# A ring of nine weight places read in place by experts in groups of three, and gate times sigmoid made before the up product's last step

## The chip, the cores and the metric

The kernel runs on one core of a Trainium2 chip. The metric is device time in microseconds of one execution; lower is better. The core has five engines with instruction streams of their own: TensorE (PE in the profile, with its weight loads as PEld), VectorE (DVE), ScalarE (ACT), GpSimd (POOL) and SyncE (SP), which here starts every transfer. Sixteen DMA engines move the data. Engines wait for each other through semaphores.

## The reference, cut to what matters

One layer: a gated delta-rule mixer and a state-space mixer side by side, an output projection, a residual, then a mixture of 32 experts over 256 tokens of width 1024, each token going to 4 experts. The change touches the experts, which are most of the time:

```python
def block_step(out, inp):                  # MoE_BLOCK rows of one expert e
    toks, gw, e = inp
    xb = t[toks]
    a = jnp.minimum(xb @ w_gate[e] + b_gate[e], SWIGLU_LIMIT)
    b = jnp.clip(xb @ w_up[e] + b_up[e], -SWIGLU_LIMIT, SWIGLU_LIMIT)
    hid = a * jax.nn.sigmoid(SWIGLU_ALPHA * a) * (b + 1)
    y = hid @ w_down[e] + b_down[e]
    return out.at[toks].add((y * gw[:, None]).astype(out.dtype)), None
```

All weights are float32, 1024 x 1024 each, three matrices for an expert.

## The kernel before, in words

Everything ahead of the experts (modulation, projections, the two mixers, the output projection, router) takes the first 427 us or so. The scratch memory is one tensor, `arena`, and `lay_out_sbuf` gives each name its place in it; places of names that are not alive together overlap.

The experts run in **turns**. A turn is a block of up to 64 rows (`SLOT`) of one expert. Every expert has at least one turn; one with more than 64 rows has further ones. The list of turns (`intab`) is made on the chip by VectorE (mark `table`), so the loops read numbers from it: entries from `BLOCKS` on hold, for each expert, the last turn of that expert. For these inputs there are 34 turns for the 32 experts: two experts have a second turn.

An expert's weights come as six **pieces** of 2048 KB: gate rows 0 to 511, up rows 0 to 511, gate rows 512 to 1023, up rows 512 to 1023, and the two halves of down. `ring` has a place for each piece, so piece n of every expert lands in place n. SyncE's loop (`pieces`, L507 to L519) waits, for each expert and piece in order, until TensorE has used that piece in the previous expert's last turn (mark `piece`, n), and then starts the transfer (L493). TensorE waits for its landing before the 16 matmuls that read it.

A turn on TensorE (`block_of_rows`, L1148 to L1193) has this order: the gate and up biases (L1156, 4 matmuls); four pieces of 16 matmuls each (L1163); the scatter of the previous turn's output into the accumulators (L1133, 8); after VectorE's `hid`, four transposes of it (L1172); the gather of the next turn's rows (L1124, 48); two transposes of the gates (L1180); the down bias (L1184, 2); two pieces of 16 (L1190). VectorE in a turn (L2239 to L2271): the selection masks of the turn ahead, then the limit on the gate product into `a` (L2259), the limit on the up product (L2261), `(up + 1) * a` (L2263), and, when ScalarE's sigmoid is there (L1544), the product with it (L2266, mark `hid`). ScalarE also copies the transposed hidden rows (L1546), the gathered rows (L1548), the gates (L1550) and the turn's output (L1552) out of the matmul banks.

TensorE, VectorE and ScalarE each have three loops over turns with one copy of the turn's code in each: turns 2 to 16, up to 15 tested turns of which `n_more` (here 2) are run and the others skipped, and the last 16. TensorE has the first turn apart. So TensorE's code holds the turn four times.

Ahead of the experts, SyncE loads the first pieces as their places come free: pieces 0 to 2 of expert 0 after the mark `mixT`, piece 3 after `low`, then the nine small copies of the biases, then pieces 4 and 5 after the last output projection.

After the last turn VectorE, ScalarE and SyncE do the last norm, the residual and the store.

Of the kernel before, what the change touches and what calls it, by code (L numbers as in the profile page):

```python
# [40 lines left out]
ARENA = 53100  # L41
LEVELS = (2, 4, 8, 16, 32)
PIECES = 6

# [43 lines left out]
class Lane:  # L88
# [23 lines left out]
    def at(self, who, *step, back=0):  # L112

        name, value = self.book.old.get((who,) + step) or self.book.new.get((who,) + step) or (f"{who}_dry", 1)
        assert self.book.dry or (who,) + step in self.book.old, (who, step)
        if name in self.book.per_old:
            value = (self.turn - back) * self.book.per_old[name] + value
        return self.sems(name), value
# [22 lines left out]
def lay_out_sbuf():  # L141
# [3 lines left out]
    def put(base, *items):  # L145
        for name, n in items:
# [6 lines left out]
    keep = put(0, ("const", NCONST), ("x", 2 * D), ("rows", 4 * D), ("cols", 8 + 20 * 5 + 8),  # L153
               ("small", 720), ("gates", 2304))
# [21 lines left out]
    put(at["WT"][0], ("yt", 4 * 512), ("mixT", KT * 256))  # L176
    put(at["kdS"][0], ("wout", KT * D))

    e = put(keep, ("h", 2 * D), ("hp", 3 * D), ("wr", 256), ("bias", 3 * 512), ("acc", 2 * D), ("hid", 6 * 512))
    assert at["wr"][0] >= at["k_tm"][0] and at["bias"][0] + at["bias"][1] <= at["xs_tm"][0]  # L180
    put(at["hid"][0], ("mix", 2 * D))
    put(e, ("hT", KT * 256))
    e = put(e, ("xcT", 512), ("hidT", 512), ("y", 512), ("GT", 256), ("Sg", 256))
    put(e, ("Sb", 64), ("route", 1500), ("ring", PIECES * 4096))
# [6 lines left out]
def layer_program(nc, book, x, ctx, consts, cc, b_ada, w_ada, wfm, wz, wsm, cols, small, wrow, w_out, w_router,  # L191
                  w_gate, w_up, w_down, b_gate, b_up, b_down, out):
    stack = ExitStack()
    with stack:
# [27 lines left out]
        rows = view(area("rows"), 4, D)  # L222
# [29 lines left out]
        brow = [xin[:, 0], rows[:, 3], xin[:, 1], area("modp", 0, D)]  # L252
# [76 lines left out]
        bst = area("v_tm", 0, D)  # L329
        b_parts = [area("v_tm", D, 512).bitcast(BF16), area("v_tm", D + 512, 512).bitcast(BF16), area("b_tm", 512, 512).bitcast(BF16)]  # L330
        dskip_eye = area("XT0", 512, 512)
        x1, hm = view(area("hid", 0, 2 * D), 2, D), view(area("h"), 2, D)
# [4 lines left out]
        acc = view(area("acc"), 2, D)  # L337
        xcT = view(area("xcT"), KT, SLOT)
        hid = view(area("hid"), 6, 512)
# [5 lines left out]
        ring = view(area("ring"), PIECES, 4, D)  # L345
        r_at = [0]
# [33 lines left out]
        passed = view(area("rows", 0, BLOCKS * 32), BLOCKS, 32)  # L380
# [26 lines left out]
        def _(sp):  # L407
# [38 lines left out]
            load("wrow", area("rows", 0, 3 * D), wrow)  # L446
# [2149 lines left out]
```

## Time and profile before

| | before |
|---|---|
| runs, us | 1397.33, 1401.47, 1409.28 |
| median | 1401.47 |
| span of the profiled execution | 1396.9 |
| TensorE busy, share of the span | 90% |
| VectorE busy | 29% |
| ScalarE busy | 19% |
| GpSimd busy | 9% |
| DMA moved | 458.59 MB, mean 328 GB/s |
| mean granted TensorE clock | 0.962 |

The profile shows one execution. The span is the time from the first to the last recorded instruction; the profiled execution has no time of its own beside it, and the lowest of the three runs is 0.4 us above the span. Busy time of TensorE counts matmuls that overlap, so a high share doesn't say that the engine is at its limit. The chain of waits is the list of steps that ended last, each with what it had to wait for; it tells who sets the pace in a stretch. Throughput in a stretch tells whether the transfers are at their limit.

### The profile page before, as it was taken

Reading aid. Unit: us, or ns where it says so; the run is one execution under the profiler, and the core shown is the slowest. Engines: PE = TensorE matmul, PEld = TensorE weight load, DVE = VectorE, ACT = ScalarE, POOL = GpSimd, SP = SyncE. Lnnn points to the kernel's source line nnn. Section 1 sums busy time; section 2 is a strip of 40 time slices with the busy share of each in tenths; the row PEclk is TensorE's granted clock in tenths of the full one; section 3 lists DMA queues with packets and bytes.
Section 4 is the critical chain, followed back from the end, with each engine's and each line's share of the span. In section 5 each row is a group of like instructions: output and inputs, shape, how many; then the busy total and the mean of one; then the engine's idle time right before and its main releaser. Section 6 shows DMA issues by size and latency. Waiting matters only on the chain.

```text
span 1396.9 us, 24933 instructions
## 1 busy us (share of the span) xinstructions
PE 1252.0 (90%) x10197; PEld 555.7 (40%) x10198; DVE 402.7 (29%) x896; ACT 260.1 (19%) x501; POOL 121.0 (9%) x168
## 2 busy tenths in 40 slices
PE   5999898568989999988999889988989999999996
PEld 2445445466654333333333333333333333333432
DVE  1265469817855121111111111111111112111112
ACT  2421432336041111111111111100000101100102
POOL 0211540185000000000000000000000000000000
PEclk9999999769988999999999999999999999999998
DMA  9958010010476999999999999999999699969994
GB/s 354 397 182 316 31 61 30 5 34 31 180 308 254 426 426 428 427 428 427 426 426 426 426 428 427 427 427 425 426 426 420 268 427 426 426 266 426 428 427 179
DMA packets 48135, 458.59 MB, mean 328 GB/s; under 512 B 4417, under 2 KB 4817, under 8 KB 22737
## 3 DMA queue, kind: packets, MB, share of 16 engines
q1 hardware_dynamic: 48080, 457.81, 79.1%
q8 instruction: 42, 0.69, 0.2%
q14 instruction: 13, 0.10, 0.0%
HBM read 456.15 MB, written 1.05 MB: 327 GB/s over the span
## 4 chain that ended last, share of the span: by engine, by line
PE 54%; DMA 34%; DVE 7%; issue 2%; ACT 1%; POOL 1%; DVEq 0%; SPq 0%; POOLq 0%; ACTq 0%
DMA arena<-in_w_up 33%; PE bank L1163 21%; PE bank L1190 8%; PE bank L673 7%; PE bank L1055 2%; PE bank L1124 2%; PE bank L584 2%; PE bank L544 1%; DVE arena L1737 1%; PE bank L1172 1%; DVE arena L2266 1%; DVE arena L2263 1%; DVE arena L2261 1%; DMA arena<-in_x 1%; PE bank L904 1%
## 5 line engine op out<-in xcount | busy, mean ns | idle before, releaser
L1163 PE MATMUL bank<-arena 128*64 128x512 f32 x2176 | 484.6, 595 | 43.7 <-DMA arena<-in_w_up 22.5
L1163 PEld LDWEIGHTS bank<-arena 128*64 128x64 f32 x2176 | 150.1, 136 | 359.3 <-issue 263.9
L1190 PE MATMUL bank<-arena 128*64 128x512 f32 x1088 | 239.2, 592 | 0.0
L2259 DVE TENSOR_SCALAR arena<-bank 128x512 f32<-128x512 f32 x34 | 23.6, 693 | 403.3 <-PE bank L1163 403.3
L1190 PEld LDWEIGHTS bank<-arena 128*64 128x64 f32 x1088 | 75.9, 136 | 140.5 <-issue 138.0
L673 PE MATMUL bank<-arena 128*128 128x512 f32 (+1 forms) x320 | 123.7, 540 | 0.0
L673 PEld LDWEIGHTS bank<-arena 128*128 128x128 f32 x320 | 60.7, 195 | 58.2 <-issue 55.3
L2190 DVE TENSOR_SCALAR arena<-arena 96x64 bf16<-96x64 f32 x35 | 8.8, 251 | 224.6 <-PE bank L1190 224.6
L1133 PE MATMUL bank<-arena 64*128 64x512 f32 x280 | 69.6, 614 | 0.8 <-ACT arena L1552 0.8
L1124 PE MATMUL bank<-arena 128*128 128x64 bf16 x1680 | 62.8, 198 | 1.1 <-DVE arena L2186 1.1
L1124 PEld LDWEIGHTS bank<-arena 128*128 128x128 bf16 x1680 | 62.9, 118 | 1.2 <-DVE arena L2186 1.2
L1544 ACT ACTIVATE arena<-arena 128x512 f32<-128x512 f32 x34 | 21.5, 632 | 219.0 <-DVE arena L2259 218.8
L1552 ACT ACTIVATE arena<-bank 128x512 f32<-128x512 f32 x34 | 20.4, 600 | 224.3 <-PE bank L1190 224.3
L1737 DVE SCALAR_TENSOR_TENSOR arena<-arena 128x512 f32<-128x512 f32 (+1 forms) x80 | 59.2, 740 | 2.8
L1544 ACT ACT_TABLE_LOAD x16 | 20.5, 1283 | 197.4 <-DVE arena L2259 197.4
L2261 DVE TENSOR_SCALAR arena<-bank 128x512 f32<-128x512 f32 x34 | 23.6, 693 | 113.1 <-PE bank L1163 113.1
L1546 ACT ACTIVATE arena<-bank 128x512 f32<-128x512 f32 x34 | 20.5, 604 | 168.6 <-PE bank L1172 168.6
L1133 PEld LDWEIGHTS bank<-arena 64*128 64x128 f32 x280 | 24.1, 185 | 45.7 <-issue 40.8
L1172 PE MATMUL bank<-arena 128*128 128x128 f32 x136 | 25.5, 310 | 11.4 <-DVE arena L2266 11.4
L1172 PEld LDWEIGHTS bank<-arena 128*128 128x128 f32 x136 | 19.1, 210 | 39.5 <-DVE arena L2266 39.5
L2248 DVE TENSOR_SCALAR arena<-arena 128x128 f32<-128x128 f32 x68 | 20.6, 346 | 42.8 <-issue 28.4
L1055 PE MATMUL bank<-arena 128*128 128x512 f32 x64 | 31.1, 643 | 0.0
(352 smaller groups left out, 1029.2 us busy)
## 6 DMA issues: line engine op xcount, KB each, us to landing
arena<-in_w_gate SPq DMA_DIRECT2D x64, 2048.0 KB, 22.5
arena<-in_w_up SPq DMA_DIRECT2D x64, 2048.0 KB, 24.1
arena<-in_w_down SPq DMA_DIRECT2D x64, 2048.0 KB, 22.0
arena<-in_w_ada SPq DMA_DIRECT2D x12, 2048.0 KB, 9.7
arena<-in_wfm SPq DMA_DIRECT2D x20, 512.0 KB, 3.4
arena<-in_wz SPq DMA_DIRECT2D x4, 1024.0 KB, 14.3
arena<-in_w_out SPq DMA_DIRECT2D x2, 2048.0 KB, 8.3
arena<-in_x SPq DMA_DIRECT2D x2, 1024.0 KB, 7.6
```

Of the source, the lines that this page charges most:

```text
L584: last = mm(ps[z_bank[m][t]], xmT[:, k, base:base + 128], ada[:, m, k, :], start=(k == 0), stop=(k == KT - 1))
L673: last = mm(dst, win[:, i % 3, k, :], cols_, start=(k == 0), stop=(k == KT - 1))
L1055: last = mm(ps[2 + 2 * t + c_], mixT[:, k, 128 * t:128 * t + 128], wout[:, k, 512 * c_:512 * c_ + 512], start=(k == 0), stop=(k == KT - 1))
L1124: last = mm(ps[7][:, SLOT * k:SLOT * k + SLOT], hparts[:, s_, t, 512 * (k // 4) + k % 4:512 * (k // 4) + 512:4], Sb[:, t, :], start=(n == ...
L1133: last = mm(ps[3 + 2 * t + c_], GT[r, t, :], ysb[r, :], start=first, stop=last_one)
L1163: last = mm(ps[m][64 * c_:64 * c_ + 64, :], xcT[:, k, :], ring[:, 2 * h_ + m, k % 4, 512 * c_:512 * c_ + 512], start=False, stop=(k == KT ...
L1172: last = nc.tensor.transpose(unit(ps[0], k), hid[:, 4, k:512:4], ident)
L1190: last = mm(ps[2][64 * c_:64 * c_ + 64, :], hidT[:, k % 4, 64 * (k // 4):64 * (k // 4) + 64], ring[:, 4 + h_, k % 4, 512 * c_:512 * c_ + 5 ...
L1544: f(hid[:, 1], hid[:, 0], ACT.Sigmoid, scale=ALPHA).then_inc(*L.mark("sig"))
L1737: v.scalar_tensor_tensor(out=dst, in0=src, scalar=convw[:, wi, tap:tap + 1], in1=dst, op0=ALU.mult, op1=ALU.add).then_inc(*L.mark("conv", i))
L2259: v.tensor_scalar(hid[:, 0], ps[0][:, :], LIMIT, None, ALU.min).then_inc(*L.mark("a"))
L2261: v.tensor_scalar(hid[:, 2], ps[1][:, :], LIMIT, -LIMIT, ALU.min, ALU.max).then_inc(*L.mark())
```

## The change: what it does

- **Ring.** There are nine places for pieces (`PLACES`): the six of `ring` and three more (`ahead0` to `ahead2`). Two of the three overlap memory that is used up to the router (`h`, `hT`; `rows`, `mix`), so the layout is rearranged: the hidden rows, the small tiles of a turn, the bias parts and the table's mask move onto constants and columns that are dead by then; `acc` and the final rows are in `ring`.
- **In place.** Piece n of expert e lands in place (6e + n) mod 9. Three experts (18 pieces) make two whole rounds, so the places repeat every three experts (`PHASES`). SyncE's and TensorE's loops go over groups of three experts (10 `GROUPS`, experts 2 to 31) with the three written out, and each reads its places directly.
- **Waits.** A piece waits for the use of the piece nine earlier: pieces 0 to 2 of an expert for pieces 3 to 5 of the expert two before, pieces 3 to 5 for pieces 0 to 2 of the expert before.
- **First pieces.** Piece 0 of expert 0 is started right after the router's weights, pieces 1 and 2 after VectorE's marks `Oss` and `gdn`, piece 0 of expert 1 after `mixT` and `Yss`; pieces 1 and 2 of expert 1 after the router's last use of the memory under them. Further ones in the loop.
- **TensorE's code.** A first turn of each expert is written out; its further turns are a test, and inside it a loop over k = 2 to 4 with a test each. TensorE reads two numbers of the table for an expert instead of one for a turn. Its three old loops go. The code holds the turn ten times, six of them in the loop over groups. VectorE and ScalarE keep their loops.
- **Sigmoid.** VectorE multiplies the limited gate product with the sigmoid before it waits for the last up piece; behind that piece come the up limit and one product, not two.
- The store reads `final`, and the load of the three norm rows is split in two.

The diff, cut to its core:

```diff
+PLACES = 9
+PHASES = 3
+GROUPS = (E_N - 2) // PHASES
...
-    e = put(keep, ("h", 2 * D), ("hp", 3 * D), ("wr", 256), ("bias", 3 * 512), ("acc", 2 * D), ("hid", 6 * 512))
...
-    put(e, ("Sb", 64), ("route", 1500), ("ring", PIECES * 4096))
+    e = put(keep, ("mix", 2 * D), ("h", 2 * D), ("hT", KT * 256), ("route", 1500), ("bias", 3 * 512), ("hp", 3 * D))
+    at["ahead2"] = (at["rows"][0] + 2 * D, 4096)
+    at["ahead1"] = (at["h"][0], 4096)
+    e = put(e, ("ahead0", 4096), ("ring", PIECES * 4096))
...
+    put(at["ring"][0] + 3 * 4096, ("wout", KT * D), ("yt", 4 * 512), ("mixT", KT * 256))
...
-            def piece(n, expert):
+            def piece(n, first, group=0):
 
                 m, c = order[n]
-                src = halves[m][bass.ds(expert, 1), c].rearrange("e p n -> p (e n)")
-                sp.dma_start(ring[:, n].rearrange("p k n -> p (k n)"), src).then_inc(sems(f"in_ring{n}"), 16)
+                place = (PIECES * first + n) % PLACES
+                src = halves[m][first:E_N:PHASES][bass.ds(group, 1), c].rearrange("e p n -> p (e n)")
+                sp.dma_start(places[place], src).then_inc(sems(f"in_place{place}"), 16)
+
+            piece(0, 0)
+            sp.wait_ge(*L.at("dve", "Oss", 1))
+            piece(1, 0)
+            sp.wait_ge(*L.at("dve", "gdn", 1))
+            piece(2, 0)
             sp.wait_ge(*L.at("pe", "mixT", 0, 1))
-            for n in range(3):
-                piece(n, 0)
+            sp.wait_ge(*L.at("dve", "Yss", 1))
+            piece(0, 1)
...
+            sp.wait_ge(*L.at("pe", "logit", 1))
+            sp.wait_ge(*L.at("act", "hparts", 0, 1))
+            sp.wait_ge(*L.at("dve", "rest", 0))
+            sp.wait_ge(*L.at("pool", "rest", 1))
+            piece(1, 1)
+            sp.wait_ge(*L.at("dve", "h", 1))
+            sp.wait_ge(*L.at("dve", "hparts", 1))
+            piece(2, 1)
...
-            def pieces(blocks, expert):
-                L.begin_turn(blocks)
-                for n in range(PIECES):
-                    sp.wait_ge(*L.at("pe", "piece", n))
-                    piece(n, expert)
+            def later_pieces(first, group, before):
+
+                for n in range(PLACES - PIECES, PIECES):
+                    sp.wait_ge(*L.at("pe", "piece", n - (PLACES - PIECES), turn=before))
+                    piece(n, first, group)
+
+            def first_pieces(first, group, two_before):
+
+                for n in range(PLACES - PIECES):
+                    sp.wait_ge(*L.at("pe", "piece", n + (PLACES - PIECES), turn=two_before))
+                    piece(n, first, group)
 
             sp.wait_ge(*L.at("dve", "table"))
-            with sp.Fori(1, E_N) as i:
-                pieces(sp.value_load(intab[0:1, bass.ds(i + (BLOCKS - 1), 1)], min_val=1, max_val=BLOCKS - 1), i)
+            later_pieces(1, 0, sp.value_load(intab[0:1, BLOCKS:BLOCKS + 1], min_val=1, max_val=BLOCKS - 1))
+            with sp.Fori(0, GROUPS) as g:
+                last = [last_turn_of(g * PHASES + n) for n in range(PHASES + 1)]
+                for n in range(PHASES):
+                    first_pieces(n + 2, g, last[n])
+                    later_pieces(n + 2, g, last[n + 1])
...
+            def further_blocks(before, last, first, group):
+
+                with pe.If(last > before + 1):
+                    with pe.Fori(2, SEQ // SLOT + 1) as k:
+                        with pe.If(last > before + (k - 1)):
+                            block_of_rows(before + k, first, group)
+                L.turn = None
...
-            with pe.Fori(2, HALF_E + 1) as i:
-                block_of_rows(i, expert_of(i))
...
-            with pe.Fori(0, MAX_MORE) as k:
-                with pe.If(n_more > k):
-                    block_of_rows(k + HALF_E + 1, expert_of(k + HALF_E + 1))
-            with pe.Fori(HALF_E + 1, E_N + 1) as i:
-                block_of_rows(n_more + i, expert_of(n_more + i))
+            last = last_turn_of(0)
+            further_blocks(0, last, 0, 0)
+            before, last = last, last_turn_of(1)
+            block_of_rows(before + 1, 1, 0)
+            further_blocks(before, last, 1, 0)
+            with pe.Fori(0, GROUPS) as g:
+                for n in range(PHASES):
+                    before, last = last_turn_of(g * PHASES + n + 1), last_turn_of(g * PHASES + n + 2)
+                    block_of_rows(before + 1, n + 2, g)
+                    further_blocks(before, last, n + 2, g)
...
-                v.tensor_scalar(hid[:, 0], ps[0][:, :], LIMIT, None, ALU.min).then_inc(*L.mark("a"))
+                v.tensor_scalar(hid[0], ps[0][:, :], LIMIT, None, ALU.min).then_inc(*L.mark("a"))
+                dve.wait_ge(*L.at("act", "sig"))
+                v.tensor_tensor(hid[3], hid[0], hid[1], ALU.mult).then_inc(*L.mark())
                 dve.wait_ge(*L.at("pe", "piece", 3))
-                v.tensor_scalar(hid[:, 2], ps[1][:, :], LIMIT, -LIMIT, ALU.min, ALU.max).then_inc(*L.mark())
+                v.tensor_scalar(hid[2], ps[1][:, :], LIMIT, -LIMIT, ALU.min, ALU.max).then_inc(*L.mark())
                 dve.wait_ge(*L.own())
-                v.scalar_tensor_tensor(out=hid[:, 3], in0=hid[:, 2], scalar=1.0, in1=hid[:, 0], op0=ALU.add, op1=ALU.mult).then_inc(*L.mark())
-                dve.wait_ge(*L.at("act", "sig"))
-                dve.wait_ge(*L.own())
-                v.tensor_tensor(hid[:, 4], hid[:, 3], hid[:, 1], ALU.mult).then_inc(*L.mark("hid"))
+                v.scalar_tensor_tensor(out=hid[4], in0=hid[2], scalar=1.0, in1=hid[3], op0=ALU.add, op1=ALU.mult).then_inc(*L.mark("hid"))
```

## Rows read from the trace of the kernel before

**Rows 1.** The page: busy tenths and throughput in 40 slices of 34.9 us.

```profile
DMA  9958010010476999999999999999999699969994
GB/s 354 397 182 316 31 61 30 5 34 31 180 308 254 426 426 428 427 428 427 426 426 426 426 428 427 427 427 425 426 426 420 268 427 426 426 266 426 428 427 179
```

**Rows 2.** Chain of waits, start and length in us: two turns paced by transfers.

```profile
543.43 3.68 PE bank L1163 x16
547.12 25.73 DMA arena<-in_w_up
572.90 3.68 PE bank L1163 x16
```

**Rows 3.** Chain of waits: turns 1 to 3, then 23 to 34 in part.

```profile
427.71 13.75 PE bank L1163 x64
...
453.93 13.76 PE bank L1163 x64
...
480.17 13.76 PE bank L1163 x64
...
1074.59 3.68 PE bank L1163 x16
...
1090.73 13.76 PE bank L1163 x64
...
1116.96 13.76 PE bank L1163 x64
...
1195.66 13.76 PE bank L1163 x64
1209.44 25.54 DMA arena<-in_w_up
1235.03 3.68 PE bank L1163 x16
...
1251.17 13.76 PE bank L1163 x64
...
1375.03 6.90 PE bank L1190 x32
```

**Rows 4.** Transfers started by SyncE before the experts, around turn 1 and around turn 24.

```profile
365.26 0.35 SPq L413 DMA_DIRECT2D arena<-in_w_router  x1
376.79 0.34 SPq L493 DMA_DIRECT2D arena<-in_w_gate  x1
...
431.62 0.35 SPq L493 DMA_DIRECT2D arena<-in_w_gate  x1
...
1057.43 3.77 SPq L493 DMA_DIRECT2D arena<-in_w_down  x2
1094.36 0.34 SPq L493 DMA_DIRECT2D arena<-in_w_gate  x1
```

**Rows 5.** Last uses of the memory under the places ahead, GpSimd and VectorE.

```profile
415.87 2.09 POOL L2505 TENSOR_TENSOR arena<-arena 128x1024 f32<-128x1024 f32 x1 [9.31 <-ACT arena L1521]
...
419.70 2.35 DVE L2168 TENSOR_TENSOR arena<-arena 128x1024 bf16<-128x1024 f32 x2
```

**Rows 6.** Timeline of turn 2 behind its last up piece.

```profile
466.49 0.63 ACT L1544 ACTIVATE arena<-arena 128x512 f32<-128x512 f32 x1
467.60 1.99 PE L1133 MATMUL bank<-arena 64*128 64x512 f32 x8
467.72 0.69 DVE L2261 TENSOR_SCALAR arena<-bank 128x512 f32<-128x512 f32 x1 [2.63 <-PE bank L1163]
469.17 0.69 DVE L2266 TENSOR_TENSOR arena<-arena 128x512 f32<-128x512 f32 x1
469.92 0.75 PE L1172 MATMUL bank<-arena 128*128 128x128 f32 x4 [0.34 <-DVE arena L2266]
```

**Rows 7.** Timeline and windows: TensorE's start of turn 19, and its granted clock.

```profile
949.57 1.07 PE L1156 MATMUL bank<-arena 96*64 96x512 bf16 x4 [6.64 <-DVE arena L2186]
...
950.64 14.72 PE bank L1163 x64
...
950.00:953.00 3.00, 3.00 (x12) 1.10 (x10) 0.00 (x0) 0.00 (x0) 0.00 (x0) 0.59 1.03 437
```

**Rows 8.** Code queue (count, MB, share): whole span, 0 to 427, 903 to 910 us.

```profile
q8 instruction: 42, 0.69, 0.2%
...
q8 instruction: 36, 0.59, 0.6%
...
q8 instruction: 1, 0.02, 1.0%
```

**Rows 9.** All queues in 480 to 903 us; busy us (x instructions) before 427.

```profile
q1 hardware_dynamic: 12397, 180.57, 100.6%
...
0.00:427.00 427.00, 356.87 (x4613) 216.59 (x4614) 240.53 (x493) 142.69 (x303) 121.01 (x168) 0.89 0.43 158
```

**Rows 10.** Chain of waits: the last up piece of turns 17, 18 and 21.

```profile
871.36 25.73 DMA arena<-in_w_up
897.14 3.68 PE bank L1163 x16
900.83 26.34 DMA arena<-in_w_up
927.21 3.68 PE bank L1163 x16
...
1015.63 3.68 PE bank L1163 x16
```

More of the change, by code:

```diff
@@ L345, in layer_program @@
         ring = view(area("ring"), PIECES, 4, D)
+        places = [area("ring", 4096 * i, 4096) for i in range(PIECES)] + [area(f"ahead{i}") for i in range(PLACES - PIECES)]
         r_at = [0]
@@ L1065, in _ @@
                     at_ = 2 * (KT * j + k)
-                    last = mm(ps[4][:, at_:at_ + 2], rows[:, row, 128 * k:128 * k + 128], ident[:, 0:2], start=True, stop=True)
+                    last = mm(ps[4][:, at_:at_ + 2], rows[row][:, 128 * k:128 * k + 128], ident[:, 0:2], start=True, stop=True)
             last.then_inc(*L.mark("rcols"))
@@ L1146, in _, with place_of, weights, landed @@
             L.stage("moe")
-            def block_of_rows(turn, expert, first=False):
+            def place_of(n, first):
+                return (PIECES * first + n) % PLACES
+            def weights(n, first):
+                return places[place_of(n, first)].rearrange("p (k n) -> p k n", k=4)
+            def landed(n, first, group):
+                return sems(f"in_place{place_of(n, first)}"), group * (2 * 16) + 16 * ((PIECES * first + n) // PLACES + 1)
+            def block_of_rows(turn, first, group, start=False):
                 L.begin_turn(turn)
@@ L1159, in block_of_rows @@
                     for m in range(2):
-                        pe.wait_ge(sems(f"in_ring{2 * h_ + m}"), expert * 16 + 16)
+                        w = weights(2 * h_ + m, first)
+                        pe.wait_ge(*landed(2 * h_ + m, first, group))
                         for k in range(4 * h_, 4 * h_ + 4):
                             for c_ in range(2):
-                                last = mm(ps[m][64 * c_:64 * c_ + 64, :], xcT[:, k, :], ring[:, 2 * h_ + m, k % 4, 512 * c_:512 * c_ + 512],
+                                last = mm(ps[m][64 * c_:64 * c_ + 64, :], xcT[:, k, :], w[:, k % 4, 512 * c_:512 * c_ + 512],
                                           start=False, stop=(k == KT - 1))
@@ L1167, in block_of_rows @@
                 pe.wait_ge(*L.at("act", "y", back=1))
-                scatter(first).then_inc(*L.mark("back"))
+                scatter(start).then_inc(*L.mark("back"))
                 pe.wait_ge(*L.at("dve", "hid"))
                 for k in range(4):
-                    last = nc.tensor.transpose(unit(ps[0], k), hid[:, 4, k:512:4], ident)
+                    last = nc.tensor.transpose(unit(ps[0], k), hid[4][:, k:512:4], ident)
                 last.then_inc(*L.mark("hidT"))
@@ L1186, in block_of_rows @@
                 for h_ in range(2):
-                    pe.wait_ge(sems(f"in_ring{4 + h_}"), expert * 16 + 16)
+                    w = weights(4 + h_, first)
+                    pe.wait_ge(*landed(4 + h_, first, group))
                     for k in range(4 * h_, 4 * h_ + 4):
@@ L1751, in row_out @@
                     dve.wait_ge(*L.own())
-                    v.scalar_tensor_tensor(out=rows[:, row, r], in0=b_, scalar=1.0 if which == 2 else 0.0, in1=rows[:, row, r],
+                    v.scalar_tensor_tensor(out=rows[row][:, r], in0=b_, scalar=1.0 if which == 2 else 0.0, in1=rows[row][:, r],
                                                  op0=ALU.add, op1=ALU.mult).then_inc(*L.mark("scaled", use))
```

73 lines of the change are left out of this document (40 added, 33 removed).

## The prediction, made before the changed kernel ran

> **What bounds the kernel now.** I read first the slices of the page: up to 427 us the transfers are mostly idle, and from slice 13 on they run at 426 to 428 GB/s, but for two slices at 268 and 266 [rows 1]. So the experts are mostly paced by weights. Then the chain of waits. In [rows 2] the last up piece of one turn starts 29.47 us after that of the turn before, and between them stands a transfer: six pieces in 29.47 us, 4.91 us each. In [rows 3] turn 24 starts 26.23 us before turn 25 (1116.96 - 1090.73) with only TensorE in the chain: TensorE alone needs 26.23 us for a turn, 3.24 less than its weights. TensorE keeps that pace from turn 24, the second one of its expert, to turn 28. In turn 29 the transfers are the limit again: from turn 28 to turn 30 it takes 1251.17 - 1195.66 = 55.51 us, 3.05 more than two turns of 26.23. From turn 30, again a second one, TensorE sets the pace to the end. So a turn without new weights builds a reserve, which then lasts about four turns.
>
> Why not longer is in SyncE's rows: after expert 22's last pieces at 1057.43 and 3.77 us later, nothing is started until 1094.36 [rows 4], since all six places are held until the second turn has used the first. The slices of 268 and 266 GB/s are (427 - 268)/427 x 34.9 = 13.0 and 13.2 us without transfers.
>
> **The change, part by part.**
>
> Three more places, filled ahead of turn 1. Before, the first place comes free at 431.62 [rows 4], with six pieces in memory. After, nine are there if those of expert 1 land in time. Their last conditions end at 415.87 + 2.09 = 417.96 and 419.70 + 2.35 = 422.05 [rows 5]; with 4.91 us of transfer each on idle queues (the page moves next to nothing there) the last lands near 430. The first piece starts right after 365.26 and not at 376.79 [rows 4]. The place that frees at 431.6 then takes the tenth piece and not the seventh, so all later landings come 3 x 4.91 = 14.7 us earlier, as long as transfers are the limit. That is so up to turn 23: TensorE alone would be through it at 427.7 + 23 x 25.9 = 1023, the weights of [rows 3] less 14.7 say 1059.9 for the last up piece that started at 1074.59. **-14.7.**
>
> Turns 24 to 34. In turn 24 the transfers have three free places for expert 23's first pieces, 14.7 us of work, and the fourth frees with the first piece's matmuls, some 4 us into it, so the 13 us of idle go. That does not count as 13 us: TensorE was already the limit there. What goes is the wait in turn 29, for the reserve is then 25.9 us, and the five turns 25 to 29 use 5 x 3.6 = 18. **-3.05.** At turn 30 it is the same; its idle time too is behind TensorE's pace.
>
> The sigmoid. In turn 2 the scatter ends at 467.60 + 1.99 = 469.59, VectorE's last product at 469.86, and the transposes start at 469.92, with 0.34 of idle [rows 6]. The sigmoid ended at 467.12, so the moved product runs to about 467.9, delays the up limit by 0.2, and `hid` is there at 469.3. The scatter now ends last. So one 0.69 us instruction less gives only the 0.3 us down to the scatter; in turns paced by TensorE 12 times (end of 23, 24 to 34). **-3.6.** If ScalarE were late, the product would sit in front of the up limit and cost instead; the sigmoid ends 0.5 us ahead of the last up piece, with a table load in it (later turns have none).
>
> SyncE. The waits moved in front of piece 1 of expert 0 up to `low` are marks that TensorE itself needs before `low`, so piece 3 and the nine bias copies aren't later; the queue ahead of them is shorter, since three pieces start up to 11 us earlier. Four table reads at a group's start delay a start while nine pieces are outstanding or landed: 0. If that cover went, in the last turns, a start would be some 2 us late with pieces landing 8 us ahead of use.
>
> TensorE's holes at the change of loops. Turn 19 begins with 6.64 us of idle, after two run and 13 skipped tests, and its four pieces take 14.72 and not 13.76, its biases 1.07, at a granted clock of 0.59 [rows 7]. That hole goes, but lies in a stretch paced by transfers: 0. VectorE and ScalarE keep theirs, with 14 us until they are needed. In its place TensorE gets two more tests in each second turn; 13 cost at least 6.64, so 0.5 each; **+1.0** for turn 24 and 30.
>
> TensorE's code. This is the unknown. Code comes in transfers of its own: 42 of 16 KB over the span, 36 of them before 427 us, where TensorE ran 4613 + 4614 instructions: one for 256 instructions [rows 8, 9]. From 480 to 903 us the loop of one turn (164 matmuls and as many weight loads, 328) goes round 14 times and no code is loaded [rows 9]. The new loop has six copies, 1968 instructions and the waits: 8 or 9 such transfers, a third of them jumped over. No row shows a loop of that size. Two costs.
> First, on the weight stream: the one code transfer in 903 to 910 us [rows 8] made the next last up piece 0.6 us late (26.34 for 25.73), and the two between turns 19 and 21 cost nothing: 1015.63 - 927.21 = 88.42 is three times 29.47 [rows 10]. If every group reloads nine, 66 up to turn 23, and they spread over the 16 engines, that is 66 x 16 KB at 427 GB/s = 2.5 us; if none, 0. I take **+1.5.**
> Second, TensorE waiting for code at a jump. Lower end 0: turn 3, entered by a jump back and a table read, starts 26.24 us after turn 2; turn 2, entered by straight code, 26.22 after turn 1 [rows 3]. Upper end: the nearest hole is turn 19's, 6.6 of idle and (14.72 - 13.76) + (1.07 - 0.6) = 1.4 of slow clock, 8.0 at the end of each group that TensorE paces, after experts 22, 25 and 28: 24. I take **+6**, two of eight each: nearer to the loop that reloads nothing, because those 0.02 us say that something covers a short wait there.
>
> Here a page speaks against the change. Only the trace's loops of 328 instructions run without a reload. The Trainium skill, Runtime: NRT & Kernel Launch, Instruction fetch mechanics, gives TensorE a first-in-first-out instruction memory of 128 KiB, filled in blocks of 16 KiB, and says that a taken branch whose target isn't in it stalls for a fetch. The trace agrees on the blocks (0.69 MB in 42), not on a window that holds the next block only. By that page the new loop would not fit and would stall at every group's end, which is the first rival's sum.
>
> **Sum.** -14.7 - 3.05 - 3.6 + 1.0 + 1.5 + 6 = -12.9 us: a span of 1384.0 against 1396.9. The median of the runs shown is 1401.47, 4.6 above that span, so **1388.6**. For the range of this case alone, the code term between 0 and 14: 1382.6 to 1396.6.
>
> **Rivals.**
>
> 1. *The loop's code is fetched again for each group, and TensorE waits for it.* For: six copies, where the trace shows only one staying. Against: the stretch before 427 us runs through 36 code transfers at that engine's full rate. The code term is then 24, and 2.5 for 1.5: 1396.9 - 12.9 + 18 + 1 = 1403.0, as a median 1407.6. No change. Even half of it would hide in turns up to 23, where each group has 3 x 3.6 = 10.7 us of slack.
>
> 2. *Slower: code transfers on the weight stream.* If nine a group all fell on the same of the 16 engines, each would cost the whole 0.6 us of [rows 10], and they would add: 66 x 0.61 = 40 us up to turn 23, against the 1.5 in the sum, so 1401.47 - 12.9 + 38.5 = 1427. It turns the sign from (12.9 + 1.5) / 66 = 0.22 us each on. Against it: the two that cost nothing.
>
> 3. *The reserve does not arise.* If the places under the router's memory were filled late, or the first free place had to wait, the stream would stay as before, and the 14.7 are lost from the sum: -12.9 + 14.7 = +1.8, 1403.3, no change. Against: 5 us of idle transfers at least ahead of 431.6.
>
> 4. *More than forecast.* No code term on either side (-7.5) and turn 1 starting 2 us or more earlier, as the bias copies land earlier: 1379 or less.
>
> **How the numbers follow.** Forecast 0.60, rival 1 0.21, rival 2 0.09, rival 3 0.06, rival 4 0.04. A measurement of this kernel tells about 1% from no change, so faster means below 1387.5 and slower above 1415.5. The forecast case lies below 1387.5 while the code term is under 4.9; I give that two thirds of it, 0.40, for the low end has the only row of a loop. Rival 4 adds 0.04: faster 0.44. Slower has most of rival 2, 0.08, and 0.01 of rival 1 with longer holes. The rest is same: 0.47. The range takes in the forecast case, rivals 1 and 3 and what rival 4 gives just below it, and leaves out most of rival 2: 1377 to 1408.
>
> **What would show it.** Nine pieces landed before 432 us, and the last up piece of every turn from about 10 to 23 starting 29.5 us after the one before, that of turn 23 near 1060. No slice of the experts' stretch below 400 GB/s until the last. From turn 24 turns of 25.9 us without a transfer in the chain. Transposes right behind the scatter. In the code queue, 42 transfers or so if the loop stays, 120 or more if it does not; then idle time of TensorE ahead of L1156 once in three experts says what a wait costs. The prediction is wrong if those holes exceed 5 us each, if the stretch up to turn 23 has turns above 30 us, or if turn 1 starts more than 3 us off 427.5.

## The result: slower, 1456.4 us, because TensorE waits for code at the end of every group

| | before | after |
|---|---|---|
| median of four runs, us | 1399.4 (1394.01 to 1409.28) | 1456.37 (1449.69 to 1458.65) |
| ratio, with its 95% interval | | 1.0396 [1.0343, 1.0448] |
| span of the profiled execution | 1396.9 | 1454.5 |
| mean granted TensorE clock | 0.962 | 0.921 |
| transfers in the code queue | 42 | 140 |

The forecast was 1388.6, the range 1377 to 1408.

First the page after, its slices (now 36.4 us each), its code queue and the chain by engine. They answer to [rows 1] and [rows 8].

```profile
PEclk9999999669969998998989989899899999899898
...
GB/s 357 366 208 270 44 58 16 33 5 80 358 232 420 425 424 422 426 424 404 424 421 401 426 394 427 421 389 425 392 425 209 371 425 424 388 170 427 354 343 30
...
q8 instruction: 140, 2.29, 0.7%
...
PE 83%; issue 8%; DVE 5%; ACT 2%; DMA 1%; POOL 1%; DVEq 0%; SPq 0%; POOLq 0%; ACTq 0%
```

The weights no longer set the pace: DMA has 1% of the chain, and from slice 13 on the throughput is below the steady 427 of before nearly everywhere, more so toward the end. "Issue", time in which the engine waited for nothing the profile shows, has 8%. The list of groups says where (busy us, mean ns | idle us ahead, releaser):

```profile
L1210 PE MATMUL bank<-arena 96*64 96x512 bf16 x136 | 25.3, 457 | 104.5 <-issue 102.5 <-ACTq L1605 1.0 <-DVE arena L2253 0.6
```

L1210 is the biases, a turn's first matmuls (L1156 before). Now one group of three experts in the chain, from one group's first turn to the next one's (start, length in us):

```profile
576.66 15.95 PE bank L1218 x64
...
604.69 13.74 PE bank L1218 x64
...
630.87 13.74 PE bank L1218 x64
...
656.30 0.61 ACT arena L1619
656.91 10.51 issue
667.42 1.07 PE bank L1210 x4
668.49 16.11 PE bank L1218 x64
```

Behind the third expert nothing runs for 10.51 us; then the biases take 1.07 and the gate and up matmuls 16.11, where they take 0.43 and 13.74 inside the group. All nine group ends look so: 10.07, 10.51, 10.70, 10.73, 11.04, 10.68, 4.97, 11.16 and 11.44 us. The 4.97 is the end whose last expert has a second turn, and a hole of 2.93 stands before expert 2's turn. The granted clock says what the slow matmuls are (windows: length, busy us of PE, PEld, DVE, ACT and POOL, granted clock, DMA share, GB/s):

```profile
566.00:575.00 9.00, 0.00 (x0) 0.00 (x0) 0.00 (x0) 0.00 (x0) 0.00 (x0) 0.57 0.99 408
576.00:580.90 4.90, 4.90 (x16) 1.61 (x14) 0.00 (x0) 0.00 (x0) 0.00 (x0) 0.50 1.01 421
581.00:584.00 3.00, 3.00 (x16) 0.98 (x14) 0.00 (x0) 0.00 (x0) 0.00 (x0) 1.00 1.02 431
```

In the hole the grant falls to the lower level, one half (0.57 is the mean of a stretch that begins before the fall), and it stays there for the first 4 us or so of the next turn's gate and up matmuls; from 581 on it is full. No engine is busy in the hole. The trace also records TensorE's jump instructions, which no row of the page counts: at a group's end the jump over the second turn's copy takes 5.9 to 6.7 us and the jump back 7.2 to 7.7, where a jump whose target is at hand takes 0.21 to 0.24. (At the end of expert 22 there is only a jump back, of 6.1 us.) TensorE itself is idle for 11.16 us (timeline):

```profile
667.42 1.07 PE L1210 MATMUL bank<-arena 96*64 96x512 bf16 x4 [11.16 <-issue]
```

The chain gives the first 0.6 us of them to ScalarE's copy of the turn's output (L1619), but this runs beside the first jump and inside a group holds no turn up, so all 11.16 belong to the code. The two jumps take 13.5: matmuls already handed to the engine run for 4.4 us beside the first one, and 1.9 us, most of it table reads, stand between the second one and the biases. Inside a group the jumps over the copy take 1.3 to 3.3 us and hold TensorE up by 0.8 us at most.

A group takes 668.49 - 576.66 = 91.83 us. Three turns without a hole are 3 x 25.83 = 77.5, so a group's end costs 14.3: 11.2 of idle TensorE, 2.9 of slow clock, and the rest in the start of the third expert's turn (630.87 - 604.69 = 26.18), behind a jump of 2.8 us. The 18 pieces of a group need 18 x 4.91 = 88.4 by their transfers. TensorE, with its stops, is slower than the weights by 3.4 us in every group, and the reserve of nine places is never used up.

The rest of the change shows as forecast. In turn 2, behind the last up piece (answers to [rows 6]):

```profile
470.58 0.63 ACT L1611 ACTIVATE arena<-arena 128x512 f32<-128x512 f32 x1
471.24 0.69 DVE L2328 TENSOR_TENSOR arena<-arena 128x512 f32<-128x512 f32 x1 [2.07 <-ACT arena L1611]
...
471.69 1.99 PE L1175 MATMUL bank<-arena 64*128 64x512 f32 x8
471.85 0.69 DVE L2330 TENSOR_SCALAR arena<-bank 128x512 f32<-128x512 f32 x1
...
472.57 0.69 DVE L2332 SCALAR_TENSOR_TENSOR arena<-arena 128x512 f32<-128x512 f32 x1
...
473.61 0.75 PE L1227 MATMUL bank<-arena 128*128 128x128 f32 x4
```

The product with the sigmoid (L2328) is done as the scatter (L1175) starts, the last product (L2332) ends at 473.26, and the transposes (L1227) start at 473.61 with no idle time ahead of them. SyncE starts the ninth piece at 423.62 and goes on as places come free (answers to [rows 4]):

```profile
366.94 0.43 SPq L509 DMA_DIRECT2D arena<-in_w_gate  x1
...
423.62 0.33 SPq L509 DMA_DIRECT2D arena<-in_w_gate  x1
435.43 0.33 SPq L509 DMA_DIRECT2D arena<-in_w_up  x1
```

**One measure for what follows.** The first gate matmul of turn 1 starts anywhere from 423.9 to 436.8 us in the profiled executions of these kernels, also in ones whose code is the same up to there but for a skipped block. A gain of a few us is lost in that. So profiled executions are compared by the span less that start: before 1396.9 - 427.71 = 969.2, after 1454.5 - 429.63 = 1024.9.

### The profile page after: what moved, and what is told of

The parts are those of the page before. It is cut to its first block, busy times and chain, and to the rows that moved or that the text cites. A ratio compares the mean times of both kernels' runs of the same rounds, so it can differ in the third digit from the quotient of the medians.

```text
span 1454.5 us, 24935 instructions
## 1 busy us (share of the span) xinstructions
PE 1270.3 (87%) x10197; PEld 568.6 (39%) x10198; DVE 401.8 (28%) x896; ACT 259.9 (18%) x501; POOL 120.8 (8%) x168
## 4 chain that ended last, share of the span: by engine, by line
PE 83%; issue 8%; DVE 5%; ACT 2%; DMA 1%; POOL 1%; DVEq 0%; SPq 0%; POOLq 0%; ACTq 0%
PE bank L1218 34%; PE bank L1246 16%; PE bank L715 7%; PE bank L1175 4%; PE bank L1166 4%; PE bank L1097 2%; PE bank L626 2%; PE bank L1227 2%; PE bank L1210 2%; PE bank L586 1%; DVE arena L1804 1%; PE bank L1239 1%; PE bank L946 1%; DMA arena<-in_x 1%; PE bank L1235 1%
## 5 line engine op out<-in xcount | busy, mean ns | idle before, releaser
L1218 PE MATMUL bank<-arena 128*64 128x512 f32 x2176 | 494.1, 613 | 0.0
L1218 PEld LDWEIGHTS bank<-arena 128*64 128x64 f32 x2176 | 160.9, 142 | 317.3 <-issue 313.1
L1246 PE MATMUL bank<-arena 128*64 128x512 f32 x1088 | 239.2, 592 | 0.0
L2326 DVE TENSOR_SCALAR arena<-bank 128x512 f32<-128x512 f32 x34 | 23.6, 693 | 496.4 <-PE bank L1218 496.4
L1246 PEld LDWEIGHTS bank<-arena 128*64 128x64 f32 x1088 | 75.9, 136 | 140.6 <-issue 138.0
L1210 PE MATMUL bank<-arena 96*64 96x512 bf16 x136 | 25.3, 457 | 104.5 <-issue 102.5
L715 PEld LDWEIGHTS bank<-arena 128*128 128x128 f32 x320 | 61.0, 195 | 58.2 <-issue 55.2
L1175 PE MATMUL bank<-arena 64*128 64x512 f32 x280 | 69.6, 614 | 0.8 <-ACT arena L1619 0.8
L1619 ACT ACTIVATE arena<-bank 128x512 f32<-128x512 f32 x34 | 20.4, 599 | 224.3 <-PE bank L1246 224.3
L1210 PEld LDWEIGHTS bank<-arena 96*64 96x64 bf16 x136 | 6.5, 119 | 130.0 <-issue 116.2
L1175 PEld LDWEIGHTS bank<-arena 64*128 64x128 f32 x280 | 24.1, 185 | 45.8 <-issue 31.1
L2328 DVE TENSOR_TENSOR arena<-arena 128x512 f32<-128x512 f32 x34 | 23.6, 694 | 47.3 <-ACT arena L1611 47.3
L586 PE MATMUL bank<-arena 128*32 128x512 f32 x192 | 25.6, 659 | 6.0 <-DMA arena<-in_w_ada 6.0
## 6 DMA issues: line engine op xcount, KB each, us to landing
arena<-in_w_down SPq DMA_DIRECT2D x64, 2048.0 KB, 14.3
```

Of the source, the lines that this page charges most:

```text
L586: last = mm(ps[bank][32 * g:32 * g + 32, :], sct[:, k, :], ada_of(use)[:, k, :], start=k < 4, stop=(k >= 4))
L715: last = mm(dst, win[:, i % 3, k, :], cols_, start=(k == 0), stop=(k == KT - 1))
L1175: last = mm(ps[3 + 2 * t + c_], GT[r, t, :], ysb[r, :], start=first, stop=last_one)
L1210: mm(ps[m][64 * c_:64 * c_ + 64, :], selb[0:96, :], bias[0:96, m, 512 * c_:512 * c_ + 512], start=True, stop=False)
L1218: last = mm(ps[m][64 * c_:64 * c_ + 64, :], xcT[:, k, :], w[:, k % 4, 512 * c_:512 * c_ + 512], start=False, stop=(k == KT - 1))
L1246: last = mm(ps[2][64 * c_:64 * c_ + 64, :], hidT[:, k % 4, 64 * (k // 4):64 * (k // 4) + 64], w[:, k % 4, 512 * c_:512 * c_ + 512], start= ...
```

## The experiments

My theory: the long loop over groups costs TensorE a wait for code at each group's end, and all else of the change works as forecast. Its rivals: the nine places or their transfers are slow in themselves; it is the jumps as such, not the loop's size; the waits are long only because the code's transfer stands behind the weights' in the DMA queues. (Letters in a quoted expectation are that expectation's own.)

### e1_three: all of the change, with TensorE's loop at half its size

```diff
+            def all_blocks(before, last, first, group):
+
+                with pe.Fori(before + 1, last + 1) as turn:
+                    block_of_rows(turn, first, group)
...
-                    before, last = last_turn_of(g * PHASES + n + 1), last_turn_of(g * PHASES + n + 2)
-                    block_of_rows(before + 1, n + 2, g)
-                    further_blocks(before, last, n + 2, g)
+                    all_blocks(last_turn_of(g * PHASES + n + 1), last_turn_of(g * PHASES + n + 2), n + 2, g)
```

> The changed kernel with TensorE's turns of an expert in one loop whose bounds are read from the table, so the loop over groups holds the turn three times and not six; places, waits, transfers and the sigmoid stay. Theory (TensorE waits for its code at the end of each group, because six copies don't stay in its instruction memory): code transfers fall from 140 to about 50, no jump is longer than 0.3 us, the holes of 10 to 11 us go, and the sum of the prediction without a code term is left plus the 1.9 us by which turn 1 starts later: a span of about 1379, ratio to the kernel before 0.985 to 0.99. Rival (the new places or the new order of transfers cost the time): holes or long turns stay, 1440 or more. Second rival (the code was all of the loss, but the reserve brings nothing): 1397.

Measured: 1376.1 us, ratio to the kernel before 0.9829 [0.9804, 0.9855]: 1.7% less than the kernel before, 5.5% less than after. In the list of groups the idle time ahead of L1210 falls from 104.5 us to 1.1, and the code queue holds 44 transfers:

```profile
L1210 PE MATMUL bank<-arena 96*64 96x512 bf16 x136 | 20.4, 379 | 1.1 <-ACTq L1608 1.0
...
q8 instruction: 44, 0.72, 0.2%
```

The chain shows what the nine places do when TensorE isn't held up:

```profile
433.52 13.73 PE bank L1218 x64
...
1025.63 39.60 DMA arena<-in_w_up
1065.27 3.65 PE bank L1218 x16
...
1081.02 13.73 PE bank L1218 x64
...
1106.85 13.73 PE bank L1218 x64
...
1339.33 6.01 PE bank L1218 x22
```

The weights set the pace up to the last up piece of turn 23, 631.75 us after turn 1; before it was 1074.59 - 427.71 = 646.88 [rows 3], so the three places bring 15.1. From there no transfer is in the chain to the end, and a turn takes 25.83. From turn 1 to the end it is 946.3 us, 22.9 less than before. The nine places are not slow, and what e1 does differently is TensorE's loop alone (its size, and that no unused copy is jumped over; e7 to e10 below separate the two).

### e2_six_ring6: the long loop alone

```diff
-            with pe.Fori(2, HALF_E + 1) as i:
...
+            with pe.Fori(0, 10) as g:
+                for n in range(3):
+                    before, last = last_turn_of(g * 3 + n + 1), last_turn_of(g * 3 + n + 2)
+                    block_of_rows(before + 1, g * 3 + n + 2)
+                    further_blocks(before, last, g * 3 + n + 2)
```

> The kernel before with the changed kernel's TensorE loop alone: groups of three experts, six copies of the turn in the loop; ring of six, old waits, old sigmoid order. Theory (code): the holes of 10 to 11 us at each group's end and a slow start of the next turn appear, about 13 us for ten groups against 9 us of slack a group that transfers give, and 15 us of lost lead at the end of each second turn, so 1440 to 1475 and about 140 code transfers. Rival (the ring is what costs): 1395 to 1405.

Measured: 1465.85 us, ratio 1.0479 [1.0446, 1.0512], 140 code transfers. The kernel before, with nothing but the six copies, has after's holes (chain):

```profile
565.47 10.44 issue
575.91 1.07 PE bank L1156 x4
576.98 15.43 PE bank L1163 x64
```

From turn 1 it is 1464.0 - 423.86 = 1040.1 us, 70.9 more than before: the loop alone does the harm. It is also 15.3 more than after, and 33 x 0.4 = 13 of that is the old order of the sigmoid (below), paid in every turn where TensorE sets the pace. That leaves some 2 us for the nine places: with this loop they bring next to nothing.

### e3_sigmoid and e5_three_oldsig: the order of the sigmoid, alone and taken out

```diff
+                dve.wait_ge(*L.at("act", "sig"))
+                v.tensor_tensor(hid[:, 3], hid[:, 0], hid[:, 1], ALU.mult).then_inc(*L.mark())
                 dve.wait_ge(*L.at("pe", "piece", 3))
                 v.tensor_scalar(hid[:, 2], ps[1][:, :], LIMIT, -LIMIT, ALU.min, ALU.max).then_inc(*L.mark())
```

e3 puts this into the kernel before; e5 puts the old order into e1.

> The kernel before with only the sigmoid's product moved ahead of the wait for the last up piece. Theory: 0.3 us less in each turn that TensorE paces (16 of 34: turns 1 to 4, 19, 20, 24 to 28, 30 to 34), of which those up to turn 20 are given back to the transfers: 2 to 4 us less, ratio 0.997 to 0.9985. Rival: nothing measurable because the scatter ends last anyway: 1.000. If the product delays the up limit when ScalarE is late: slower by up to 0.7 us a turn.

> The kernel with three copies (e1_three), with the old order of VectorE's part: the product with the sigmoid last. Theory: the turns that TensorE paces (24 to 34 and the first ten) take 0.3 to 0.4 us more, the others nothing; 11 turns behind the stretch paced by transfers make 3 to 5 us: 1380 beside 1376. Rival (the order is covered here too): no difference to e1_three.

Measured: e3 1396.27 us, ratio 0.9975 [0.9955, 0.9996]; e5 1379.74 us, ratio to the kernel before 0.9879 [0.9854, 0.9905]. From turn 1: e3 967.5, 1.7 less than before; e5 1377.1 - 424.90 = 952.2, 5.9 more than e1, 1.3 of it a slow clock in its turn 1 (15.02 for 13.73). The chain of e5 shows the turn of the old order, 26.24 us, against e1's 25.82 (1106.85 - 1081.02 = 25.83 above):

```profile
1073.92 13.76 PE bank L1218 x64
...
1100.16 13.76 PE bank L1218 x64
```

That is 0.4 us a turn where TensorE sets the pace. In e3 most of it is given back: TensorE comes to the weights' limit one turn earlier, in turn 28 and not in 29, and once more at the end.

```profile
1168.91 13.76 PE bank L1163 x64
1182.69 23.50 DMA arena<-in_w_up
1206.23 3.68 PE bank L1163 x16
```

### e6_three_ring6: the short loop, nine places, but the waits of a ring of six

```diff
-                    first_pieces(n + 2, g, last[n])
-                    later_pieces(n + 2, g, last[n + 1])
+                    all_pieces(n + 2, g, last[n + 1])
```

The three pieces of expert 1 that are started ahead wait for turn 1 as well.

> The kernel with three copies, its nine places in use, but each piece waits for the piece six earlier as in a ring of six, and expert 1's first three pieces aren't loaded ahead of turn 1. Theory (the reserve of three pieces is what e1_three gains): two gaps of 13 us in the transfers come back, the last up piece of turn 23 starts 14.7 us later, and the transfers stop a part of the last turns once more, 15 to 20 us in all: 1392 to 1398. Rival (what e1_three gains is the removed hole between TensorE's loops): 1376 to 1380.

Measured: 1400.47 us, ratio 1.0019 [0.9998, 1.0039]. Its slices on the page have both dips of [rows 1] again (263 and 272 GB/s), where e1 has 427 at the first and 348 at the second:

```profile
GB/s 355 395 181 315 31 61 30 4 34 7 296 214 216 425 427 426 428 427 427 427 428 427 427 427 427 429 427 426 427 428 427 263 427 427 427 272 423 427 427 184
```

From turn 1 it takes 1400.1 - 432.06 = 968.0, 21.7 more than e1: so much is the reserve worth. What is left, 1.2 us under before, is the sigmoid as in e3.

### e4_hint: the same long loop, its jump back announced

```diff
-            with pe.Fori(0, GROUPS) as g:
+            with nc.Fori(0, GROUPS, engines=[mybir.EngineType.PE], hint_back_edge=True) as g:
```

> The changed kernel with a prefetch hint for the jump back of the loop over groups, set at the head of each round. Theory: the jump back (7.2 to 7.7 us in the changed kernel) falls below 1 us if the hint's code is kept, the forward jump ahead of it (5.9 to 6.7 us) stays, so the hole at a group's end shrinks from 10.7 to about 4 us: 1395 to 1415. Rival: a round is longer than what the memory holds, so what the hint brought at its head is gone at its end: unchanged at 1455.

Measured: 1436.81 us, ratio 1.0268 [1.0241, 1.0296], 131 code transfers. The jump back falls to 5.5 to 6.2 us, the jump ahead of it stays at 6.0 to 6.4, and the hole at 9 (chain):

```profile
580.22 15.20 PE bank L1218 x64
...
659.68 9.13 issue
668.81 1.06 PE bank L1210 x4
669.88 14.75 PE bank L1218 x64
```

A group takes 669.88 - 580.22 = 89.7 and not 91.8 us. Where both jumps are missed, the announcement takes off a sixth of a group end's cost. At the end of expert 22, where the second turn's copy runs and no long jump stands ahead of the jump back, it takes off nearly all: the jump back takes 1.10 us for 6.13, and the hole is gone (chain; 4.97 in after):

```profile
1135.37 0.22 issue
1135.59 0.62 PE bank L1210 x4
```

So a jump back that is missed alone can be covered by announcing it; why that fails behind another miss isn't shown.

### e7_spare1, e8_spare2, e9_fit, e10_shift: how long a loop may be

e1's loop has some 1055 of TensorE's instructions, the one of after some 2090 (counted in the compiled program; e1's trace records 1048 in a round). These kernels put into e1's loop copies that never run. Each was run once.

```diff
                     all_blocks(before, last, n + 2, g)
+                    if n < 1:                      # e8: n < 2
+                        with pe.If(last > BLOCKS - 2):
+                            block_of_rows(before + 2, n + 2, g)
+                    if n == 1:                     # e9 and e10 only
+                        with pe.If(last > BLOCKS - 2):
+                            gather()
+                            gather()
```

e10 also has one skipped `gather()` ahead of the loop.

> The kernel with three copies plus one copy of the turn that is skipped in each group: the loop is about 1400 instructions long, 5.5 code transfers of 256. Theory (an instruction memory of fixed size, larger than this loop): code transfers stay near 44 to 50, no hole, a span as e1_three within run-to-run differences of the first 430 us. Rival (each jump over code costs, whatever the size of the loop): a wait of 3 to 6 us at the skipped copy in every group, over 100 code transfers.

> The same with two skipped copies: about 1740 instructions, 6.8 code transfers. If the memory holds 2048 instructions and keeps what it has, as e7_spare1. If blocks ahead are loaded too and push older ones out, the loop reaches over 8 blocks of 256 and one more is loaded ahead: the jump back waits 6 to 7 us and code transfers rise above 100.

> The kernel after with three copies of the turn in TensorE's group loop, and beside them copies that never run (one of the turn, two of the gather of 48 matmuls), some 1590 instructions in all, between the 1400 of the version with one spare copy (1376.9 us) and the 1740 of the one with two (1450.9). Theory A (what the memory keeps is seven or eight blocks of 256 instructions with the one loaded ahead): by count this loop still lies in seven blocks; about 1377, under 60 code transfers in the span, no idle time of over 1 us ahead of the biases' matmuls. Theory B (the limit is simply a count of instructions somewhere above 1400): 1377 or 1450, without preference.

> The same loop as the one before it, but pushed about 100 instructions later in TensorE's code by one gather that is skipped ahead of the loop, so that by count it lies in eight blocks and not in seven. Theory A (blocks, counted with where the loop begins): waits at every group again, 1440 to 1455 and over 120 code transfers. Theory B (a count of instructions, wherever the loop begins): the same time as the run before, within 5 us.

| | loop, instructions | time, us | span from turn 1 | code transfers |
|---|---|---|---|---|
| e1 | 1055 | 1376.1 | 946.3 | 44 |
| e7 | 1400 | 1376.9 | 947.5 | 46 |
| e9 | 1590 | 1375.0 | 948.3 | 46 |
| e10 | 1590, 100 later | 1388.0 | 949.3 | 47 |
| e8 | 1740 | 1450.9 | 1021.7 | 128 |
| after | 2090 | 1456.4 | 1024.9 | 140 |

The single times of e9 and e10 are 13 us apart, but turn 1 starts at 424.86 in the one and at 436.82 in the other, and from there they differ by 1.0; why turn 1 starts later isn't known. So e10 has no holes, and the finer theory, that blocks of 256 counted from where the code begins decide, falls, at least as I had counted them. What stands is that up to 1590 instructions nothing is loaded again and that at 1740 nearly everything is. That is a step, not a slope: 150 more instructions cost 73 us, 350 on top of them 3.

e8 also shows the two waits apart, since its jumps over a spare copy and its jump back do not stand together (chain):

```profile
625.52 3.10 issue
628.62 1.06 PE bank L1210 x4
629.68 16.34 PE bank L1218 x64
...
658.33 3.45 issue
661.78 0.79 PE bank L1210 x4
662.57 15.26 PE bank L1218 x64
```

Each wait that leaves a hole is 5.9 to 6.5 us long by the trace's record of the jump, and the holes are 3.1 to 3.8 us long. Yet a group here takes 662.57 - 571.25 = 91.3 us, as in after: two holes of some 3.3 us each bring their own stretch of slow clock.

### e11_nodma: the long loop without the weights' transfers

```diff
-                for n in range(PHASES):
-                    first_pieces(n + 2, g, last[n])
-                    later_pieces(n + 2, g, last[n + 1])
...
-                        pe.wait_ge(*landed(2 * h_ + m, first, group))
+                        if first < 2:
+                            pe.wait_ge(*landed(2 * h_ + m, first, group))
```

> The kernel after with its six copies, but no weights are transferred behind expert 1: all later experts compute with stale weights, so that the only large transfers of the experts' stretch are gone and code alone uses the DMA engines. Theory A (each wait for code is long because its transfer stands in queues that the weights fill): the same 130 to 140 code transfers, but holes at a group's end of under 4 us instead of 10 to 11; 34 turns of 25.8 and 10 holes of 3 give 1357 + 30, about 1350 to 1390. Theory B (a wait costs this much by itself): holes stay at 10 to 11 us and the pieces after them at 15.6 to 16.1, so the time stays at 1445 to 1460.

Measured: 1399.08 us in one run. The code queue holds the same 140 transfers, and the holes are half as long (chain):

```profile
568.27 16.38 PE bank L1214 x64
...
648.58 5.43 issue
...
655.07 15.65 PE bank L1214 x64
...
q8 instruction: 140, 2.29, 0.7%
```

A group takes 655.07 - 568.27 = 86.8 us, so its end costs 9.3 and not 14.3. The jump ahead takes 3.3 to 3.7 us and the jump back 4.7 to 5.0. Neither theory of the expectation had it: the full queues make about half of the hole, the other half is there on empty ones, and the slow clock costs nearly the same either way. Since 86.8 is below the weights' 88.4, I estimate that on queues that served code first the long loop would cost little up to turn 23 and still lose 9 us at every later group end; no run shows it.

## Why the prediction was wrong

**The step that failed** is the last of the sum, TensorE waiting for code: +6, between 0 and 24. Measured: turn 1's gate matmuls to turn 34's are 1414.03 - 429.63 = 984.4 us in after, and 33 turns of 25.83 are 852.4, so TensorE's own stops are 132.0. Of them 100.8 are TensorE's idle time at the nine group ends and before expert 2 (94.2 of it in the "issue" rows of 2.93 us and more), 24.3 the slow clock behind the group ends, 2.3 that of turn 1, and 4.3 late starts of a group's third expert, up to 0.8 us each behind a jump of 2.6 to 3.2 us. In e1 the same stretch takes 1339.33 - 433.52 = 905.8, with 53.4 us of waiting for weights in it. The stops swallow these, and the term is 132.0 - 53.4 = 78.6 where I took 6 and bounded by 24 (with the terms for added tests and for code on the weight stream, 8.5). Turn 24 divides it (chain of after, turns 24 and 34):

```profile
1117.75 13.74 PE bank L1218 x64
...
1414.03 13.73 PE bank L1218 x64
```

From turn 1 to turn 24 after takes 688.1 us and e1 647.5 (1081.02 - 433.52): 40.6 arose where I had put nothing. From turn 24 to turn 34 it is 296.3 against 258.3: 38.0 for the three ends that I had counted.

Three things in that term were wrong, in order of weight:

1. *Its stretch.* "Even half of it would hide in turns up to 23, where each group has 3 x 3.6 = 10.7 us of slack." It did hide 53.4 us, but the stops up to turn 24 come to 53.4 + 40.6 = 94.0, since a group's end costs 14.3, more than the slack of its own group. And the slack is not there in the first groups: the nine places' reserve carries TensorE at its own pace to about turn 9 (e1 is 53.4 us behind that pace at turn 24, which is 15 turns at 3.6), so every stop there is paid in full. I counted three group ends where nine count.
2. *Its size.* The nearest row was turn 19's hole of 6.64 us and 1.4 of slow clock [rows 7]. A group's end has two missed jumps in sequence, one over the second turn's copy and one back, each on a DMA system that the weights fill. So it is 11.2 + 2.9 us, against 8.0; the three ends were 38.0 and not 24.
3. *Whether it occurs.* I put 0.60 on a loop that mostly stays, from 0.02 us at one entry to a loop and a stretch without reloads. Both were rows of a loop of 328 instructions. That turn 3 started on time at [rows 3] said that a jump back whose target is near costs nothing; it says nothing about one whose target is 2000 instructions back. Here I should have given more weight to what I had cited. The Trainium skill, Runtime: NRT & Kernel Launch, Instruction fetch mechanics, has 128 KiB for TensorE and a stall where a taken branch's target isn't in the current window of two blocks. At 16 KB for 256 instructions [rows 8, 9], 2090 instructions are 131 KB, and for after the trace agrees with the stall: 140 transfers for 42. A window of two blocks the runs don't show: loops of 1055 to 1590 instructions load nothing again. And the 1740 of e8 would fit in 128 KiB and are loaded again all the same; the runs put the edge between 1590 and 1740.

Rival 1 was thus the right mechanism at a chance of 0.21 with a wrong price: its 24 us assume waits in three groups. The condition that I had written for being wrong, "if those holes exceed 5 us each", is met at eight of nine group ends, and at the ninth with 4.97.

**What was right**, on e1. Three places: forecast -14.7 up to turn 23, measured -15.1, the sigmoid and turn 1's noise included. No wait in turn 29 and the sigmoid: forecast -3.05 - 3.6 = -6.65; from turn 23's last up piece to the end e1 takes 1379.8 - 1065.27 = 314.5, before 1396.9 - 1074.59 = 322.3: -7.8. The difference is the sigmoid, 0.4 us a turn (26.23 to 25.83) where I had 0.3. In sum, the forecast without its terms for tests and code is -21.4, and e1 has -22.9. For the reserve alone the forecast has -17.75, and e1 against e6 shows 21.7, since without the reserve most of the sigmoid's gain is given back to the weights, as in e3. The tests (+1.0) cost nothing by themselves: in after turn 31, which has the tests of expert 27's second turn ahead of it, starts 1322.01 - 1296.19 = 25.82 us after turn 30, as any turn without a stop does. Those of expert 22 stand ahead of the missed jump back and are part of that stop.

**Code on the weight stream**, +1.5: after has 104 code transfers behind turn 1's start, and at 0.8% of 16 engines' time there the queue takes next to nothing from the weights. As TensorE sets the pace, it cost nothing. Rival 2, which made all of the loss of it, gave the time nearest to the result, by the wrong mechanism: in e11, without a weight stream, the holes stay.

**Left open.** Why e8's loop of 1740 instructions is loaded again and one of 1590 is not, wherever it begins. And which part of the jumps' 3.3 to 5.0 us on empty queues is the transfer itself and which is TensorE's taking up of the new code. And why the announced jump back is covered when it is missed alone and hardly behind another miss.

## What to carry to other kernels

Before a loop body is written out several times, count the instructions of its busiest engine: here TensorE's loop ran free up to 1590 and lost 14 us at each pass from 1740 on, whatever the copies did. A copy that never runs counts as much as one that does; a loop with bounds read from a table held the same rare second turn at half the code. And before a stop is counted as hidden in slack, compare the whole stop, with its slow clock, with the slack between two stops, and ask from which turn on that slack exists: what the change itself builds as a reserve takes the slack of the first turns away.

## What the runs showed of the hardware that I had not expected

- At a group's end a missed jump takes 5.9 to 7.7 us while the weights fill the DMA engines and 3.3 to 5.0 us while they are idle; a hit takes 0.21 to 0.24. Of the two misses of a group's end, or of a single one in e8, 2.0 to 2.4 us leave TensorE no idle time.
- The cost in clock doesn't grow with the hole. Behind a hole of 3.10 us the granted clock was 0.50 for 6.2 us and the next 64 matmuls took 16.34 us for 13.73 (e8); behind one of 2.26 us they took 15.43 (e11, end of expert 22); behind those of 10 and 11 us 14.82 to 16.11. So two short holes can be dearer than one long one of the same sum. But behind the hole of 2.93 us before expert 2's turn in after they took 13.74: the length of a short hole doesn't say alone whether the clock falls.
- Announcing the jump back took some 1.8 us off it behind another miss, and 5.0 us where it was missed alone; it took nothing off the jump ahead (e4).
